# Last block's entry in three weight units, its squares added on GpSimd, the gates' products ahead of the factors' row, and a delta rule with folded key factors

## What is computed

```python
hn = rms_norm_2(x, w_norm)
proj = hn @ w_in                      # q_a k_a v_a z_a b_a a_a q_b k_b v_b z_b
q_a, k_a, v_a = split(silu(causal_depthwise_conv([q_a, k_a, v_a])))   # width 4
q_a = l2_norm(q_a) * DK**-0.5;  k_a = l2_norm(k_a)
beta = sigmoid(b_a);  g = -exp(a_log) * softplus(a_a + dt_bias)
o_a = gated_delta_rule_chunked(q_a, k_a, v_a, g, beta)                # 4 heads of 128
o_a = rms_norm_2(o_a) * silu(z_a)
q_b, k_b = rope(rms_norm_2(q_b)), rope(rms_norm_2(k_b))
o_b = diff_attention(q_b, k_b, v_b, lam);  o_b = rms_norm_2(o_b) * silu(z_b)
x = x + concat(o_a, o_b) @ w_out
```

## Time and profile before

| | us |
|---|---|
| median of 3 runs (lowest, highest) | 1112.38 (1107.86, 1114.41) |
| the profiled execution: its own time | 1112.99 |
| the profiled execution: span on the core | 1111.5 |
| TensorE (PE) busy | 1069.7 (96%) |
| VectorE (DVE) busy | 648.9 (58%) |
| ScalarE (ACT) busy | 434.7 (39%) |
| GpSimd (POOL) busy | 88.5 (8%) |

### The profile page before, as it was taken

One profiled execution on the slowest core, in us unless ns is written; L12 is line 12 of the kernel. 1 busy time (PEld: TensorE's weight loads), 2 busy tenths in 40 slices (PEclk: granted clock), 3 DMA queues, 4 the chain that ended last, 5 costly groups with the idle time before them and its releaser, 6 DMA issues.

```text
span 1111.5 us, 15358 instructions
## 1 busy us (share of the span) xinstructions
PE 1069.7 (96%) x6244; PEld 845.4 (76%) x6244; DVE 648.9 (58%) x1118; ACT 434.7 (39%) x767; POOL 88.5 (8%) x76
## 2 busy tenths in 40 slices
PE   7999999999999999999999999988999999997998
PEld 5777777778788888888888888867677777875676
DVE  5645454556437788777772212653667567576574
ACT  6233232344443544444442222442344354254431
POOL 1000000000210000000000000001020120120210
PEclk9999999999999999999999999988999999999999
DMA  8221213122331333333323233121111111110102
GB/s 329 79 89 59 95 57 95 58 76 78 111 95 57 96 114 106 103 96 96 96 93 102 88 114 114 44 89 38 58 58 39 59 57 58 58 38 25 53 20 75
DMA packets 25429, 90.78 MB, mean 82 GB/s; under 512 B 2880, under 2 KB 3136, under 8 KB 25232
## 3 DMA queue, kind: packets, MB, share of 16 engines
q1 hardware_dynamic: 23328, 83.90, 23.9%
q0 software_dynamic: 592, 3.61, 0.9%
q10 hardware_dynamic: 1440, 2.31, 0.6%
HBM read 87.71 MB, written 2.10 MB: 81 GB/s over the span
## 4 chain that ended last, share of the span: by engine, by line
PE 82%; DVE 8%; ACT 5%; issue 3%; POOL 1%; DMA 1%; SPq 0%; ACTq 0%; DVEq 0%; POOLq 0%
PE PS L508 22%; PE PS L511 21%; PE PS L509 21%; PE PS L543 4%; DVE Wl L1028 1%; ACT Wh L1697 1%; PE PS L634 1%; PE PS L763 1%; PE PS L1001 1%; PE PS L998 1%; PE PS L999 1%; PE PS L647 1%; DVE Yc L1067 1%; PE PS L657 1%; ACT P L2001 1%
## 5 line engine op out<-in xcount | busy, mean ns | idle before, releaser
L508 PE MATMUL PS<-Hh,Wh 128*128 128x512 f32 x856 | 352.7, 412 | 0.6 <-ACT M L1817 0.6
L511 PE MATMUL PS<-Hh,Wl 128*128 128x512 f32 x856 | 336.9, 394 | 0.0
L509 PE MATMUL PS<-Hl,Wh 128*128 128x512 f32 x856 | 336.5, 393 | 0.0
L1028 DVE TENSOR_TENSOR Wl<-raw,Wh 128x1024 fp32r<-128x1024 f32 x155 | 191.6, 1242 | 189.8 <-ACT Wh L1697 188.3
L508 PEld LDWEIGHTS PS<-Hh,Wh 128*128 128x128 f32 x856 | 162.5, 190 | 43.7 <-issue 11.0
L1697 ACT ACTIVATE Wh<-raw 128x1024 fp32r<-128x1024 f32 x155 | 161.4, 1051 | 71.8 <-PE PS L511 60.9
L511 PEld LDWEIGHTS PS<-Hh,Wl 128*128 128x128 f32 x856 | 162.2, 189 | 35.4
L509 PEld LDWEIGHTS PS<-Hl,Wh 128*128 128x128 f32 x856 | 162.6, 190 | 30.6 <-issue 1.4
L508 PE MATMUL PS<-Ah,Wh 128*128 128x512 f32 x176 | 69.8, 396 | 0.0
L509 PE MATMUL PS<-Al,Wh 128*128 128x512 f32 x176 | 69.8, 396 | 0.0
L511 PE MATMUL PS<-Ah,Wl 128*128 128x512 f32 x176 | 69.8, 396 | 0.0
(11 more groups left out here) (313 smaller groups left out, 1485.8 us busy)
## 6 DMA issues: line engine op xcount, KB each, us to landing
raw<-in_w_units SPq DMA_DIRECT2D x155, 512.0 KB, 3.5
relb<-in_rel POOLq DMA_DIRECT2D x1, 2048.0 KB, 9.4
out<-X ACTq DMA_DIRECT2D x8, 256.0 KB, 2.1
X<-in_x SPq DMA_DIRECT2D x3, 512.0 KB, 7.9
X<-in_x SPq DMA_DIRECT2D x2, 256.0 KB, 4.2
raw<-in_w_units SPq DMA_DIRECT2D x2, 256.0 KB, 4.5
rope<-in_rope POOLq DMA_DIRECT2D x1, 512.0 KB, 4.2
mats<-in_mats POOLq DMA_DIRECT2D x1, 448.0 KB, 3.5
```

The costliest lines, as they stand in the source:

```text
L508: pe.matmul(bank, Wh[:, s, w], rhs[0](r), start=first and j == 0, stop=False)
L509: pe.matmul(bank, Wh[:, s, w], rhs[1](r), start=False, stop=False)
L511: ins = pe.matmul(bank, Wl[:, s, w], rhs[0](r), start=False, stop=last and end)
L1028: dv.tensor_tensor(Wl[:, s, :], raw[:, s, :], Wh[:, s, :].bitcast(F32), sub).then_inc(unit_split, 1)
```

## The change

1. **Entry.** Three units (`c0`, `c1`, `c2`) run with the tiles, the third one tile behind (`LAGS_LAST`). Its result goes to PSUM bank 6.
2. **Squares.** TensorE's L562 products are gone. GpSimd adds the eight square tiles with seven additions of 128x512 into `ssum`; four products with ones (`norm_columns`) follow on TensorE.
3. **Gates' rows.** Their 24 products stand behind these four, with `norm_row` in their midst (ahead of the last nine). VectorE copies the gates' rows right behind its reads of `c0` and `c1`; `c2` is read inside the gates' chain.
4. **Stage 0** has eight units, in the order `z0`, `z1`, `v`, `Kr`, `Qb`, then the three `c` of head 1. The gates' rounds have paces of their own.
5. **Folded delta rule.** The matrix is formed from the raw keys: its factors beta/(sum of squares + eps) (`key_w`) are multiplied into the decay matrix DT once, by one more DVE operation. Gone: the row of beta, its mask `Bm`, the row of key factors, the scaled keys, the second product on LT, `beta_eg`. New small ones of 128x4: a reciprocal, `key_w`, `key_end`. Values are scaled by a column `key_norm` (power +1/2, GpSimd). Keys times keys comes ahead of the values' turn, and the keys' turn and queries' product move from level 1 to level 2.

```diff
-PACE_SCALARS, PACE_END = 3, 1.5
-PACE_SCORES, PACE_PREP = (None, 1.9, 1.9, 1.25), (1.5, 1.7, 1.7, 0.8)
+PACE_GATES, PACE_END = (2, 3, 3, 5, 5, 2, 1), 1.5
+PACE_SCORES, PACE_PREP = (None, 1.9, 1.9, 1.25), (1.35, 1.7, 1.7, 0.8)
...
+STAGE_UNITS = [[(a, x) for x in (("z0", "z1", "v", "Kr", "Qb") if a == 0 else
+                                 ("v", "Kr", "Qb", "z0", "z1"))] for a in range(GH)]
+for a in range(GH - 1):
+    STAGE_UNITS[a] += [(a + 1, x) for x in ("c0", "c1", "c2")]
...
-    LAGS_START, LAGS_UP, LAGS_LAST = (0, 4, 5), (0, 0, 1, 1), (0, 0)
+    LAGS_START, LAGS_UP, LAGS_LAST = (0, 4, 5), (0, 0, 1, 1), (0, 0, 1)
...
# TensorE
-                if squares is not None and m < KT:
-                    pe.wait_ge(*norm_sq.at(turn, m))
-                    for t in range(NT):
-                        ins = pe.matmul(PS[:, 3, t:t + 1], squares[:, m, tok(t)], ones[:],
...
-        def gate_chain(st):
+        def gate_products():
             pe.wait_ge(*lam_dv.at(0, "ba_lo"))
             for k in range(KT):
+                if k == KT - 3:
+                    norm_row(2)
...
-            row_of(b7, beta[:, i, :]).then_inc(*prep_pe.tick(i, "b"))
...
-            row_of(b6, rqk[:, 0:NT]).then_inc(*prep_pe.tick(i, "kr"))
...
-        units_together(U_P2, G_P2, LAGS_LAST, 2, up_squares)
-        norm_row(2)
+        units_together(U_P2, G_P2, LAGS_LAST, 2)
+        norm_columns(2)
+        gate_products()
...
# VectorE, prep
-            dv.tensor_tensor(tiles(Bm[:]), tiles(b7), over_tiles(mat(K_STRICT_T)),
-                             mult).then_inc(*prep_dv.tick(i, "bm"))
...
-            dv.tensor_tensor(CK, CK, b6, mult).then_inc(*prep_dv.tick(i, "kn"))
...
+            dv.reciprocal(key_inv[:], rqk[:, 0:NT]).then_inc(*prep_dv.tick(i, "inv"))
+            dv.tensor_tensor(key_w[:], beta[:, i, :], key_inv[:], mult).then_inc(*prep_dv.tick(i, "w"))
+            dv.tensor_tensor(key_end[:], to_end[:, i, :], key_w[:], mult)
+            dv.tensor_tensor(tiles(DT[:]), tiles(DT[:]), over_cols(key_w[:]),
+                             mult).then_inc(*prep_dv.tick(i, "dtw"))
...
-            dv.tensor_tensor(LT[:], b7, DT[:], mult).then_inc(*prep_dv.tick(i, "lt0"))
-            dv.tensor_tensor(LT[:], LT[:], Bm[:], mult).then_inc(*prep_dv.tick(i, "lt"))
+            dv.tensor_tensor(LT[:], b6, DT[:], mult).then_inc(*prep_dv.tick(i, "lt"))
...
# GpSimd
+        for k in range(1, KT):
+            gp.wait_ge(*norm_sq.at(2, k))
+            if k > 1:
+                gp.wait_ge(*last_add.at(0, k - 1))
+            gp.tensor_tensor(ssum[:], ssum[:] if k > 1 else up_squares[:, 0, :], up_squares[:, k, :],
+                             add).then_inc(*last_add.tick(0, k))
         norm_factors(2)
```

More of the change, by code:

```diff
@@ L64 @@
 N_COLS = C_GNORM + 4
-(K_ID, K_UPPER, K_HALVES, K_SWAP, K_NEG_T, K_STRICT_T, K_LEVEL) = range(7)
+(K_ID, K_UPPER, K_HALVES, K_SWAP, K_NEG_T, K_LEVEL) = range(6)
 BLK, N_LEVELS = 32, 7
+KQ_LEVEL = 2
 N_MATS = K_LEVEL + 2
@@ L230, in program @@
     beta = sb("beta", [P, GH, NT])
-    beta_eg = sb("beta_eg", [P, GH, NT])
+    eg = sb("eg", [P, GH, NT])
+    key_inv, key_norm, key_w, key_end = (sb(f"key_{n}", [P, NT]) for n in ("inv", "norm", "w", "end"))
+    plus_half = sb("plus_half", [P, NT])
     to_end = sb("to_end", [P, GH, NT])
@@ L318, in program @@
     norm_add = steps("norm_squares", [("add", k) for k in range(1, KT)])
+    last_add = steps("last_norm_squares", range(1, KT))
     norm_hh, norm_sq = steps("norm_high", range(KT)), steps("norm_squares_done", range(KT))
@@ L370, in program @@
     levels = range(1, N_LEVELS)
[L371 to L374, removed]
+    prep_pe = steps("prep_tensor", ["g", "sums", "kk", "vt", *(
+        x for lv in levels for x in (("y", lv), ("t", lv), *(("kt", "qk") if lv == KQ_LEVEL else ()))),
+        "u", "w"])
+    prep_dv = steps("prep_vector", ["d", "dt", "ms", "inv", "w", "dtw", "lt", "strips",
+                                    "m0", "tt", "ti", "lm", "vb", *(
         x for lv in levels for x in (*((("tt", lv),) if lv < 5 else ()), ("t", lv),
                                      *(("t64",) if lv == 4 else ()),
-                                     *(("kd", "at", "rq") if lv == 1 else ()))), "wt"])
+                                     *(("kd", "at", "rq") if lv == KQ_LEVEL else ()))), "wt"])
     decay_ac = steps("decays_scalar", ["eg", "dt"])
@@ L1312, in vector_program @@
             behind(j)
-        for n in range(U_DOWN + RING, U_DOWN + N_DOWN + AHEAD):
+        for n in range(U_DOWN + RING, U_P2 + 3):
             split(n)
@@ L1860, in scalar_program @@
                     round_unit(U_DOWN + 3 * k + m + AHEAD)
+            if k == KT - 1:
+                round_unit(U_P2 + 2)
             squares(1, k, U_DOWN + 3 * k + 2, M2, C_FFNPOST)
         def gate_chain(st):
-            yield from idle(4)
+            yield from idle(3)
             ac.wait_ge(*gate_dv.at(0, "ba"))
@@ L1924, in prep @@
                 yield from idle(3)
-            yield from idle(7)
+            yield from idle(3)
             ac.wait_ge(*prep_dv.at(i, "lt"))
@@ L2143, in gate_chain @@
         def gate_chain(st):
-            yield from idle(7)
+            yield from idle(6)
         def prep(st, i):
@@ L2152, in prep @@
             gp.wait_ge(*prep_dv.at(i, "ms"))
-            gp.tensor_tensor(rqk[:, 0:NT], rqk[:, 0:NT], half[:, 0:NT],
+            gp.tensor_tensor(key_norm[:], rqk[:, 0:NT], plus_half[:],
                              power).then_inc(*prep_gp.tick(i, "rk"))
@@ L2156, in prep @@
                              power).then_inc(*prep_gp.tick(i, "rq"))
-            yield from idle(8)
+            yield from idle(7)
             while st.scanning:
@@ L2268, in _layout @@
     big = np.concatenate([w2[:, :n], w2[:, n + 2 * GH:]], axis=1)
-    p2 = _units(np, big).reshape(8, GH, P, KT, P)[[0, 1, 2, 6, 5, 4, 3, 7]]
-    p2 = p2.transpose(1, 0, 2, 3, 4).reshape(32, P, KT, P)
+    p2 = _units(np, big).reshape(8, GH, P, KT, P)
+    part = {n: j for j, n in enumerate(("c0", "c1", "c2", "z0", "Qb", "Kr", "v", "z1"))}
+    p2 = np.stack([p2[part[x], a] for a, x in sorted(UNIT_PLACE, key=UNIT_PLACE.get)])
     wout = _units(np, inp["w_out_2"][0])
```

114 lines of the change are left out of this document (54 added, 60 removed).

## The result

| | before | changed |
|---|---|---|
| median of 19 runs, us (lowest, highest) | 1111.66 (1107.86, 1115.09) | 1106.19 (1103.73, 1108.38) |
| profiled execution, us; span | 1112.99; 1111.5 | 1107.15; 1105.7 |

The ratio is 0.995, with a 95% interval of 0.9937 to 0.9962: 5.5 us faster, where 14 to 15 were forecast, and 0.2 us outside the range (1089 to 1106).

What follows compares the result with a forecast made beforehand. TensorE, busy 96% of the span, was taken to bound the kernel. Entry +1.3, stage 0 -13.6 and stages 1 to 3 -2.6 sum to -14.9 us from 1113.0, giving 1098 us, range 1089 to 1106.

Steps and rivals of the forecast that it cites:

- The step that failed: Stages 1 to 3: two rows less in each, -2.6 us, with waits and clock unchanged; moved steps -4 to +5.
- (a): Entry, TensorE: eight groups of squares go, 0.79 us each, -6.3 us.
- (b): Entry, TensorE: 24 products of c2 come in at 0.23 us each, +5.6 us.
- (c): Entry: GpSimd's additions hold back VectorE's X and Hl by 3.3 us, bounds nothing to 6.5.
- (d): Entry's end: seventh addition ends at about 725.4; TensorE waits some 2 us; four ssum products take half of 0.79 us.
- (e): Entry's end: 24 gate products and factors' row take 6.1 us; the first 15 cover epsilon, power and TensorE's 1.3 us wait.
- (k): GpSimd's power pair: 1.01 us each as now, hidden; powers do not shut out VectorE, so nothing counted for its work beside them.
- Rival 1: Entry: the additions do not hinder VectorE, so it ends 3.4 us earlier, total 1094.6 us; chance 0.15.
- Rival 2: Stage 0: no new wait at the inverse's first copy, -2.5 and -2.1 us, total 1093.5; chance 0.17.
- Rival 3: More waits: powers shut out VectorE, stages 1 to 3 wait up to 3 to 5 us more; about 1103; chance 0.12.
- Rival 4: Entry and half of stage 0: TensorE stays at 1.2 GHz, slower than before, up to 1129 us; chance 0.04.
- Rival 5: Entry: squares stay exposed, it ends at 734, a 4 us wait drops the clock; 1102 to 1103 us; chance 0.07.

Runs made afterwards that it cites:

- The last kernel, with four edits: Changed kernel with c1's taps early, queries' product at level 1, Kr of head 0 weighted later and Vb a round earlier: 1088.99 us, ratio 0.9800.

## Why the prediction was wrong

**The step that failed** is "Waits and clock there I take as they are; moved steps make this -4 to +5" for stages 1 to 3. They changed by +8.0, where -2.6 stood in the sum, and that is outside these bounds. The move of the queries' product to level 2 was known as a part of the change, and got no term. I worked through the new order of stage 0 instruction by instruction, and did not do the same for the stages with a scan, although the order there was as easy to read. Three things were to be seen in it: L770 behind a level-2 result of which VectorE's reading stands behind the scan's last work; 8 triples without rounds at a stage's end; Vb behind the scores' maxima. The waits cost +4.2 us net. The second omission is in the bound: a clock loss of 8.5 us stood in neither end of it. In stage 0 I had counted a long wait at about twice its length, and in stages 1 to 3 not at all. With level 1 in place of level 2 the changed kernel takes 1097.5 us, which is the forecast of 1098; stages 1 to 3 are then 228.1 us, forecast 228.5. That agreement is partly luck: these stages then have 1.3 us less idle time than before and 3.4 us more clock loss, and what is left fell by 5.1 us, about twice what the two rows were to give.

Step by step, against the changed kernel's trace:
- (a), (b) TensorE's own work in the entry: -6.3 + 5.6 + 0.4 = -0.3 us forecast, -1.3 measured (24.6 busy before; 23.3 with one addition). Two sizes were off. A tile's squares cost 0.91 us, not 0.79 (groups start 2.28 us apart, less six products at 0.23). And the four products with `ssum` are listed as eight instructions, like a tile's squares, and took 0.81 us, not 0.4.
- (c) VectorE held back: 3.3 us forecast, 4.2 measured (18.0 - 13.8); by the run with one addition 3.3 to 4.2. Both engines lose in turn, as assumed, but Hl loses 1.04 and X 0.38. Rival 1, no hindrance, is out.
- (d) TensorE's wait of 2 us behind the seventh addition did not come. The waits lie in the tiles instead, 2.3 us in all. The addition ended at 722.4, 19.2 us after the entry's start (forecast 20.6), when the last products of `c2` still ran.
- (e) The gate products covered epsilon and power: no wait at the row of factors, though the power took 1.93 us and not 1.01 (rows under (k)).
- Entry +1.6 (forecast +1.3). Terms that were off by about 1 us each way cancel in it, (a) and (b) against (c), so a hit this close is luck.
- Stage 0 -13.8 (forecast -13.6). Within it: `glog` 0.6 (0.7), `LmT` 0.7 (0.7), first copy 2.2 (2.5), no wait for `rqk`. Rival 2 is out. This sum too hides two errors that cancel: idle time fell by 4.9 us, forecast 3.9, and TensorE's own work by about 5.5, forecast 5.6 + 0.9 = 6.5. The clock loss is 3.4 (2.1), but of 6.8 and not of 5.3: the second stretch of low clock in the kernel before runs from 764.9 to 771.8 us (clock 0.51). It began inside the wait of 4.7 us, not behind it.
- (k) The power pair. POOL and DVE:

```profile
755.50 1.01 POOL L2167 TENSOR_TENSOR key_norm<-rqk,plus_half 128x4 f32<-128x4 f32 x1 [27.63 <-DVE rqk L1378]
...
755.85 0.68 DVE L1388 TENSOR_TENSOR head_DT<-head_DT,key_w 128x512 f32<-128x512 f32 x1
```

VectorE's multiplication ran inside the power at its usual length, in all four heads. By the rule of the Trainium skill, "SBUF — State Buffer", section "Who interferes with whom", it would have stood until the power was done. That rule holds here for the additions (and for splits and products, 2.28 us), and not for a multiplication that begins some 0.4 us into a power of 128x4. It does hold for the other order, a power that begins behind VectorE's operation. DVE and POOL at the end of the entry:

```profile
725.01 1.22 DVE L1032 TENSOR_TENSOR Wl<-raw,Wh 128x1024 fp32r<-128x1024 f32 x1
...
725.18 1.93 POOL L2104 TENSOR_TENSOR rstd<-rstd,half 128x4 f32<-128x4 f32 x1 [2.80 <-DVE rstd L1061]
```

The same power took 1.01 us in the kernel before, with no split beside it. For the order that (k) was about, taking the row over the rule was right.

- Rival 3 named the right place, the waits of stages 1 to 3, but with the wrong mechanism (powers) and less than half the price. Rival 4 (TensorE at 1.2 GHz through the entry) is out: the clock there is 1.00. Rival 5 is out: the four products with `ssum` did not wait for GpSimd, and the entry ended at 730.7, not at 734.

**What stays open.** What brings a stretch of low clock. Level 1 took 5.5 us of idle time and 5.1 us of clock loss out of stages 1 to 3, but the two do not go together in all runs. With the taps early the idle time fell by 4.3 us and the clock loss rose from 11.9 to 13.6. The last kernel, with four edits, has 6.6 us of idle time and loses 8.5 us there, the kernel before has 12.2 and loses 3.4. The same 2.2 us wait was followed by low clock in one run and not in the other, and stage 3 differed by 5 us between kernels that are the same there. So half of what level 2 cost is waits with a known cause. That its waits brought the low clock, the other half, is argued, not shown.

## What to carry to other kernels

When a chain gets shorter in a kernel whose engines work through interleaved lists, read the new order in every stage that uses the chain, for the engine that is not the bound: what now stands between a result and its reader. Place a product whose bank must first be read by VectorE behind a result that is long done, not behind a fresh one. And work handed to an idle GpSimd is not free where VectorE's operations have both inputs in SBUF: here seven additions of 1.3 us cost VectorE 4.2 us, about what it needs to make them itself (7 x 0.60 us from start to start).

## What was not expected

A small operation can be stretched as much as a large one. In the run with queries at level 1, DVE and POOL:

```profile
837.53 1.15 DVE L1548 TENSOR_TENSOR nmax<-nmax,rqk_b 128x2 f32<-128x2 f32 x1
...
837.37 1.29 POOL L2177 TENSOR_TENSOR head_QG<-C,ssum 128x512 f32<-128x512 f32 x1 [19.29 <-PE PS L770]
```

The same happened once more, at 918.03 us; its 14 other instances take 0.16 us. From 700 us on, low clock comes in stretches of 3.4 or 6.8 us at half the clock, 1.7 us lost for each 3.4, and several times with TensorE fully busy and no wait of 0.3 us or more in the 14 us ahead (956 us in the kernel before, 864 us in the changed one).
